# Entry of the down projection in two FFNs: the last gated rows split from their stage, and one unit's weights loaded earlier

## What is computed

```python
def swiglu_half(x, pre, post, w_gate, w_up, w_down):
    h = rmsnorm(x, pre)
    y = (jax.nn.silu(h @ w_gate) * (h @ w_up)) @ w_down
    return x + 0.5 * rmsnorm(y, post)
```

## Time and profile before

| | us |
|---|---|
| median of 3 runs | 3129.38 |
| the runs | 3135.6, 3123.69, 3129.38 |
| span of the profiled execution | 3135.0 |
| TensorE busy with matmuls | 2961.5 (94%) |
| VectorE, ScalarE, GpSimd busy | 1799.3, 1132.7, 789.6 |
| mean granted clock of TensorE | 0.972 |

### The profile page before, as it was taken

How to read it: one execution, slowest core, us unless ns; L and a number is a source line. 1 busy time by engine, 2 the same in 40 slices (tenths; PEclk the granted TensorE clock), 3 DMA queues, 4 the chain that set the end, 5 groups by cost and what they waited for, 6 DMA issues and landing times. The chain is left out here.

```text
span 3135.0 us, 65632 instructions
## 1 busy us (share of the span) xinstructions
PE 2961.5 (94%) x27498; PEld 2800.8 (89%) x27498; DVE 1799.3 (57%) x2864; ACT 1132.7 (36%) x2182; POOL 789.6 (25%) x884
## 2 busy tenths in 40 slices
PE   8999998998999988979999989999998999999998
PEld 8999998998999978838777579999998999999998
DVE  7777764565545546566554552343425877775445
ACT  5333333343112223344665351221234433333433
POOL 3555451023001123230003000000025555552003
PEclk9999999998999999989999999999998999999999
DMA  6556667554422120011016641112123466666753
GB/s 173 187 178 196 186 206 240 166 176 137 131 75 62 55 90 4 18 28 47 11 46 180 218 170 45 47 51 54 31 77 112 140 196 191 200 194 192 228 180 110
DMA packets 417279, 393.90 MB, mean 126 GB/s; under 512 B 50616, under 2 KB 368353, under 8 KB 416218
## 3 DMA queue, kind: packets, MB, share of 16 engines
q1 hardware_dynamic: 383962, 277.57, 29.7%
q0 software_dynamic: 31984, 112.13, 11.0%
q10 hardware_dynamic: 1040, 0.00, 0.0%
HBM read 284.11 MB, written 105.53 MB: 124 GB/s over the span
## 5 line engine op out<-in xcount | busy, mean ns | idle before, releaser
L2146 PE MATMUL banks<-hid_pieces,dn_high 128*128 128x258 f32 x2464 | 454.0, 287 | 21.3 <-DVE hid_pieces L2088 21.3
L1908 PE MATMUL banks<-x_pieces,up_pieces 128*128 128x258 f32 x3360 | 416.5, 284 | 0.7 <-DVE sq L2002 0.7
L1908 PE MATMUL banks<-x_pieces,gate_pieces 128*128 128x258 f32 x3360 | 415.3, 283 | 0.9 <-ACT sq L1944 0.8
L1908 PEld LDWEIGHTS banks<-x_pieces,up_pieces 128*128 128x128 f32 x3360 | 410.6, 190 | 1.1 <-DVE sq L2002 1.1
L1908 PEld LDWEIGHTS banks<-x_pieces,gate_pieces 128*128 128x128 f32 x3360 | 408.8, 189 | 1.7 <-ACT sq L1944 1.4
L2146 PEld LDWEIGHTS banks<-hid_pieces,dn_high 128*128 128x128 f32 x2464 | 386.2, 192 | 22.8 <-DVE hid_pieces L2088 21.0
L2146 PE MATMUL banks<-hid_pieces,dn_part 128*128 128x258 f32 x1232 | 349.6, 284 | 0.0
L1167 PEld LDWEIGHTS banks<-XG,pR 128*128 128x128 f32 (+1 forms) x1800 | 286.0, 189 | 10.4 <-issue 6.1
L1167 PE MATMUL banks<-XG,pR 128*128 128x344 f32 (+1 forms) x1800 | 291.4, 323 | 3.7 <-DVE pR L2681 2.9
L1167 PE MATMUL banks<-XR,mg_gate 128*128 128x344 f32 x1728 | 283.3, 319 | 1.3 <-PEq L53 1.3
L1167 PEld LDWEIGHTS banks<-XR,mg_gate 128*128 128x128 f32 x1728 | 273.9, 188 | 1.6 <-issue 1.6
(11 more groups left out here) (565 smaller groups left out, 5502.0 us busy)
## 6 DMA issues: line engine op xcount, KB each, us to landing
hid_spill<-h_stage SPq DMA_DIRECT2D x44, 516.0 KB, 4.0
chain_slot<-hid_spill POOLq DMA_DIRECT2D x64, 258.0 KB, 3.8
t_sums<-chain_slot POOLq DMA_DIRECT2D x64, 258.0 KB, 3.0
dn_low<-w_sums SPq DMA_DIRECT2D x32, 384.0 KB, 3.6
praw<-in_w_in SPq DMA_DIRECT2D x24, 512.0 KB, 4.3
sq<-in_w_in SPq DMA_DIRECT2D x24, 512.0 KB, 4.1
chain_slot<-in_ffn_down POOLq DMA_DIRECT2D x46, 256.0 KB, 4.4
w_sums<-chain_slot POOLq DMA_DIRECT2D x46, 256.0 KB, 3.2
```

Source lines behind the costliest of these rows:

```text
L1908: ins = k.nc.tensor.matmul(out, self.w[m][:, a, w, f * P:(f + 1) * P], self.x[p][:, b, x, f * TQ:(f + 1) * TQ], start=first and f == 0 and ...
L2146: ins = k.nc.tensor.matmul(k.ps[2 * j + q][:, 0:TQ], a[s][:, f * P:(f + 1) * P], k.hid_pieces[m % 2][:, q, f, b, :], start=m in self.FRESH ...
```

## The change

Three things, in both FFNs (they share the class).

1. Product 0 gets other parts (`H_FIRST`): rows 0-4 and 5-9 of the first quarter, 0-5 and 6-9 of the second, and as fifth part, `TAIL`, row 10 of both quarters. The tail is not loaded: `hidden_high` and `hidden_low` split it from `h_stage`, where the gated product stands, in one instruction of 128x516 each. Its order on ScalarE and VectorE is ahead of the second quarter's parts, behind the two of the first.
2. On SyncE the wait for the store of the last pair's first half is gone; all four parts are loaded before it (the two of the second quarter after the fourth product of problem 42, then unit 1's weights, then the store). Ahead of unit 4's weights, which go where the stage lies, SyncE also waits until the tail's low half is made.
3. Unit 5's weights are loaded after unit 2, ahead of the wait for the block sums and part 4 of product 1.

```diff
+    H_FIRST, TAIL = ((0, 0, 5), (0, 5, 10), (1, 0, 6), (1, 6, 10), (0, 10, 11)), 4
...
     def load_hidden(self, sp, m, i):
-        q, a, b = self.H_PARTS[i]
+        q, a, b = self.h_parts(m)[i]
...
         for i in range(2):
             self.load_hidden(sp, 0, i)
+        self.product[4].wait(sp, self.last - 4)
+        for i in range(2, 4):
+            self.load_hidden(sp, 0, i)
+        self.load_down(sp, 1)
         self.store_hidden(sp, it, 0)
-        self.product[4].wait(sp, self.last - 4)
-        self.load_hidden(sp, 0, 3)
-        self.load_down(sp, 1)
 
     def sp_down(self, sp, between):
-        self.hid_stored.wait(sp, 2 * self.N - 1)
-        self.load_hidden(sp, 0, 2)
-        self.load_hidden(sp, 0, 4)
         self.product[4].wait(sp, self.last - 3)
         self.load_down(sp, 2)
         self.load_down(sp, 3)
...
         self.hid_stored.wait(sp, 2 * self.N)
+        self.hid_low.wait(sp, self.h_order(0).index(self.TAIL) + 1)
         self.load_down(sp, 4)
         self.unit_done(sp, 1)
         for i in (2, 3):
             self.load_hidden(sp, 1, i)
+        self.unit_done(sp, 2)
+        self.load_down(sp, 5)
         self.chain_sums.wait(sp, 4 * self.CHAIN)
         self.chain_stored[2].wait(sp, self.CHAIN)
         self.load_hidden(sp, 1, 4)
         for u in range(5, self.LOADED):
-            self.unit_done(sp, min(u - 3, 23))
-            self.load_down(sp, u)
+            if u > 5:
+                self.unit_done(sp, min(u - 3, 23))
+                self.load_down(sp, u)
...
         if n == self.last:
-            for i in (3, 2, 4):
+            for i in (4, 2, 3):
                 self.hidden_high(act, 0, i)
...
         if n == self.last:
-            for i in (3, 2, 4):
+            for i in (4, 2, 3):
                 self.hidden_low(dve, 0, i)
...
+    def h_parts(self, m):
+        return self.H_PARTS if m else self.H_FIRST
+
+    def tail(self, part):
+        return self.k.hid_pieces[0][:, :, self.HALF - 1, part, :]
+
+    def staged_tail(self):
+        return self.hs[:, 0, 0:2 * TQ].rearrange("p (q t) -> p q t", q=2)
+
     def hidden_high(self, act, m, i):
-        q, a, b = self.H_PARTS[i]
-        self.hid_landed[i].wait(act, m + 1)
+        if m == 0 and i == self.TAIL:
+            self.gated(act, self.last - 1, 2)
+            self.product[4].wait(act, self.last - 4)
+            self.hid_high.done(self.k.nc.scalar.activation(self.tail(0), self.staged_tail(), ACT.Copy))
+            return
+        q, a, b = self.h_parts(m)[i]
+        self.hid_landed[i].wait(act, m if i == self.TAIL else m + 1)
...
     def hidden_low(self, dve, m, i):
-        q, a, b = self.H_PARTS[i]
+        q, a, b = self.h_parts(m)[i]
         self.hid_high.wait(dve, 5 * m + self.h_order(m).index(i) + 1)
+        if m == 0 and i == self.TAIL:
+            self.hid_low.done(self.k.nc.vector.tensor_tensor(self.tail(1), self.staged_tail(), self.tail(0).bitcast(F32),
+                                                             ALU.subtract))
+            return
...
     def h_order(self, m):
-        return (0, 1, 3, 2, 4) if m == 0 else (0, 1, 2, 3, 4)
+        return (0, 1, 4, 2, 3) if m == 0 else (0, 1, 2, 3, 4)
```

More of the change, by code:

```diff
@@ L2141, in unit_pe @@
                 for f in range(first, end):
-                    for part, (hq, a, b) in enumerate(self.H_PARTS):
+                    for part, (hq, a, b) in enumerate(self.h_parts(m)):
                         if j == 0 and (hq, a) == (q, f):
```

## The result

The changed kernel took 3111.94 us (median of 5 runs, 3107.82 to 3113.0), the kernel before beside it 3134.43: a ratio of 0.9929, with a 95% interval of 0.9913 to 0.9945, or 17 to 27 us. That is faster by more than the 0.5% that can be told here, and inside the predicted range of 3094 to 3115, but 8.9 us above the predicted 3103.0 and just above the 3097 to 3110 that the prediction gave its own account.

The account below looks back on a forecast made before the run. TensorE bounds the kernel, idle 21.3 us ahead of down products for hidden rows. Holes worth 31.4 us, less 3.0 of waits left and 2.0 of chain slip, give 26.4: 3129.4 becomes 3103.0 us, range 3094 to 3115.

Parts of the forecast that it names:

- the four: TensorE's waits in units 0 and 4 of both FFNs, with half clock behind: 7.0 + 5.7 + 8.6 + 10.1 us.
- Hole 1: Unit 0, ahead of row 9 of the first quarter: late rows 9 and 10; closing it gains 7.0 and 5.7 us.
- Hole 2: Unit 4, rows 9 and 10 of the second half: splits behind unit 5's late weights; closing gains 8.6 and 10.1 us.
- What is late next: Unit 4: the last part of hidden rows, held by POOL's last sum, leaves waits of 1.2 and 1.8 us.
- The slip of the sums' chain: Unit 5's early loads delay POOL's last sum chain by 0 to 3 us per FFN; 1.0 taken.
- No clock drop behind a wait of 2 to 3 us: Behind the wait left in unit 4 TensorE keeps full clock; 0 taken, bounds 0 and 2.8 us per FFN.
- B: Unit 5's early weights collide with the sums, chain slips 3 us, clock falls; gain 16.8 us, 3112.6; chance 0.14.
- A: The prediction's own account: holes closed, waits of 1 to 3 us left in unit 4; 3097 to 3110 us, chance 0.70.
- C: In unit 4, parts issued at 504.17 or unit 5's weights still land late; gain only 12.7 us, 3116.7; chance 0.07.
- D: Tail in unit 0 split no sooner than its loaded copy and SyncE still stands; 3129 us, chance 0.03.
- E: Slower: last sum chain's three transfers take 8.8 us each, slip 16.5 us, loss 10.2 us, 3139.6; chance 0.03.

Follow-up runs that it names:

- e4: The changed kernel, with GpSimd making the last row pair's block sums from h_stage instead of from rows stored and loaded back; 3100.83 us, ratio 0.9896.
- e1: The changed kernel with unit 5's weights again behind the wait for the block sums, so only the tail and new load order; 3125.68 us, ratio 0.9971.
- e3: The changed kernel with parts 2 and 3 of product 1's hidden rows split at unit 3 ahead of unit 5's weights; 3113.49 us, ratio 0.9937.
- e6: The changed kernel with the tail loaded from device memory and split behind the second quarter's first part; 3123.04 us, ratio 0.9964.
- e2: The kernel before, with only unit 5's weights moved ahead of the wait for the block sums; 3119.58 us, ratio 0.9964.
- e5: The kernel before, with only the last row pair's block sums made by GpSimd from the stage in SBUF; 3115.87 us, ratio 0.994.

## Why the prediction was right, and where it was not

**What the holes were worth.** The prediction had 31.4 us for the four. e4, where all are closed, gains 30.4 in the down parts: right to 1 us.

**Hole 1 closed by the tail from the stage: right.** There is no wait in unit 0 (after, e1, e3, e4), and it comes back when the tail is loaded again (e6). The predicted sequence holds as well: stage split without a wait, and 1,290 KB landed in time for the second quarter. VectorE came to the tail's low half at 482.84; forecast was 481.07, and this profile's down part started 1.85 us later than that of before (481.62 against 479.77).

**Hole 2 at row 9 closed by unit 5's weights: right** (e2 has it closed, e1 does not), with the issue at 506.98, forecast for 505 plus those 1.85.

**What is late next: right in place, too small in price.** The prediction put a wait at row 6 of the second quarter, with 1.2 + 1.0 = 2.2 us in the first FFN and 1.8 + 1.0 = 2.8 in the second, and the clock at 1.00 behind it. Measured were 3.53 and 4.02 us, and above the floor of e4 6.3 and 6.1 us: 12.4 for both instead of 5.0, which is 7.4 of the 8.4 us by which the 18.0 fall short of 26.4 (the other 1.0 is that between 31.4 and 30.4). Two terms of the sum failed: of the 7.4, about 2.5 are waits that are longer than forecast, and 4.9, the larger share, is the half clock behind them.

*The slip of the sums' chain, taken as 1.0 us per FFN and as a matter of transfers alone.* From the store of the last pair's second half to SyncE's issue of the last part, 24.5 and 24.7 us passed before, and 26.6 and 26.8 after: 2.1 in each. The transfers do make up about what was taken for them: from the issue of the first loads to the first sum 7.95 us passed instead of 6.90, and 7.56 instead of 7.36; from the issue of the fourth load to the last sum 3.46 instead of 3.41, and 4.67 instead of 3.89. That is 1.1 us in the first FFN and 1.0 in the second. But in the first FFN it is not due to unit 5's weights: the time at the first loads is 8.03 in e1, which has these weights late, and 7.98 in e2, where nothing ahead of those loads was changed, so why it was 6.90 before stays open. What can hang on the weights is the fourth load, which took 3.38 and 3.40 in e1 and, with the weights early, 3.97 and 4.94 in e2: here it adds 0.05 and 0.8.

The other part of the slip is GpSimd's arithmetic, which the sum held constant (in the first FFN 0.4 us of it is made up for, since the first loads go out that much sooner after the store): its last sum took 2.76 us instead of 1.30 in the first FFN, and in the second the first sum 2.10 and the last 1.71, instead of 1.30 and 1.29. Each of these long sums stands beside an operation of VectorE on SBUF: at the last sums it is part 3 of the hidden rows, whose split now begins at 513.57 where before it came after 526, at the first sum of the second FFN a split of weights. e3 tells the two apart: with VectorE's split moved away, the last sum takes 1.30 and the slip is 1.4 and 1.2 us; the waits of TensorE shrink by 0.9 and 1.0.

*No clock drop behind a wait of 2 to 3 us.* Behind 3.53 and 4.02 us the clock fell, and behind the 2.67 and 3.01 of e3, where GpSimd's last sum has its usual length, it fell too. Behind 2.29 us (e2), near the 2.2 that was forecast for the first FFN, it stayed. So at the length that was forecast the drop could go either way, and taking none had no more behind it than the row with 1.41 us. The upper bound of the term, 2.8 us per FFN, was near: 6.3 - 3.53 = 2.8 and 6.1 - 4.02 = 2.1. Counted from the clock it is more, half of the 6.2 us at 0.50, so 3.1 in each; the second figure is lower since the norm's later wait (5.73 us here, 6.04 in e4) and the half clock behind it were together about 1 us shorter here than in e4.

**The rivals.** Of the five accounts it is B, not the prediction's own A, that came nearest in time (3112.6 against 3111.94 measured) and in its signs (waits of 4.2 and 4.8 us, and half clock behind them). A's sign, a wait of 1 to 3 us at a clock of 1.00, is in neither FFN, and a sign against it, a wait of over 4 us with half clock behind it, is in the second. That the time still fell into the stated range is due to the room that the range left for B. But B has the cause wrong in part: it laid 3 us per FFN on the transfers, whose part was 1 (of its two rows, 3.3 and 6.4 us, the first is a load and the second a store). C is out: the two parts that had been asked for were in time. D is out by the rows of unit 0 and e6. E is out: the chain slipped 2.1 us, and a loss began at 11.4.

**The total.** 18.0 us is what the profiles show of the change itself; the medians differ by 22.5, with an interval that holds both. The time came out 8.9 us above the forecast: 8.4 for the terms above, 5.1 because the median of before was 3134.43 in these runs instead of 3129.38, less the 4.5 us by which the medians differ more than the down parts. That the last two nearly cancel is luck.

## What to carry to other kernels

When a value that was just computed goes to device memory and straight back, look first for every reader that could take it from where it stands. Here that gained 8.0 us for TensorE's operand alone (e1), 19.6 for GpSimd's sums alone (e5), and 30.4 with both (e4, which has unit 5's weights early as well). Once the sums were early, TensorE had no wait in unit 4 with these weights early (e4) or late (e5). When an edit moves work of one engine forward, list what the other engines do at its new time: VectorE's split did not get longer, it made GpSimd's sum longer, on the chain that came next. And price a wait that is left on TensorE with the half-clock stretch that rows show behind waits of its length.

## What the runs showed of the hardware that was not expected

**VectorE and GpSimd take turns.** In the changed kernel the slow last sums end 1.16 us after VectorE's operation, in both FFNs: 513.74 + 2.76 = 516.50 against 513.57 + 1.77 = 515.34 in the first, and in the second

```profile
2876.60 1.71 POOL L1753 TENSOR_TENSOR sq<-sq,chain_slot 128x516 f32<-128x516 f32 x1 [3.58 <-DMA sq<-hid_spill]
...
2875.38 1.77 DVE L2109 TENSOR_TENSOR hid_pieces<-hid_raw,hid_pieces 128x1548 fp32r<-128x1548 f32 x1 [0.35 <-ACT hid_pieces L2098]
```

2878.31 against 2877.15. In the first FFN of e2 it is 517.36 + 2.26 = 519.62 against 516.69 + 1.77 = 518.46, again 1.16, and in the second FFN of e6, with a sum of 2.89 us, it is 1.15. So the sum did next to nothing until VectorE was through, however much of VectorE's operation was left, and then ran for most of its usual 1.30. In e3, where the sum was first (509.48 against 509.95), VectorE was the one that took longer. The Trainium skill (SBUF — State Buffer, section SBUF: two separate sides) describes this as an exclusive lock: a VectorE operation with two SBUF inputs and a GpSimd operation that reads SBUF hold a shared pair of ports for the whole instruction, and the one that comes second is blocked. The traces agree, with these numbers; the prediction did not weigh that rule.

**The clock behind short waits.** Twelve waits of TensorE of up to about 4 us can be set beside the granted clock of the windows behind them. It stayed at 1.00 behind waits of 1.41, 1.75 (e6), 2.29 (e2, unit 4 of the second FFN) and 2.91 us (e2, unit 0), and fell to 0.50 behind 2.67 and 3.01 (e3), 2.91 and 3.61 (e5), 3.50 and 3.66 (e2), and 3.53 and 4.02 (after). Between 2.67 and 2.91 us both happened, and the two waits of 2.91 us stand at the same place of the program (unit 0 of the first FFN); what decides there stays open. Nor does the length of the wait alone say what the fall costs. Half of the time that products ran at 0.50 is lost: 1.4 us behind 3.50 (e2) and 2.91 (e5), 1.7 behind 2.67 and 3.01 (e3), and 3.0 to 3.1 behind 3.53, 3.61, 3.66 and 4.02.
